# One inference step of a hybrid decoder trunk: the prompt tile with channel-wise projections, two hT buffers, V as loaded operand, probabilities divided on GpSimd

## What is computed

```python
mod = silu(c) @ w_mod + b_mod                      # shift, scale, gate
h = rmsnorm(x, norm_pre) * (1 + scale) + shift
proj = h @ w_in                                    # 1024 -> 2880
qa, ka, va, ga, pb, gb, xc, gc = split(proj)
q, k = rope(qa), rope(ka)                          # A: 8 heads, 2 kv heads, width 64
ya = swa_banded(q, k, va, sinks) * silu(ga)        # window 128, blocks of 128
yb = rwkv7_time_mix(pb, gb, ...)                   # B: 4 heads x 64, delta rule
yc = rglru_mix(xc, gc, ...)                        # C: width 256, conv 4, recurrence
y = concat(ya, yb, yc) @ w_out                     # 1024 -> 1024
x = x + gate * rmsnorm(y, norm_post)
```

## Time and profile before

| | us |
|---|---|
| median of 3 runs | 3261.7 |
| lowest, highest | 3260.98, 3263.45 |
| the profiled execution, its own time | 3271.33 |
| its span (first to last instruction) | 3269.5 |
| DVE busy in it | 1750.7 |
| ACT busy in it | 1429.8 |

### The profile page before, as it was taken

One profiled execution on the slowest core, in us unless ns is written; L12 is line 12 of the kernel. 1 busy time (PEld: TensorE's weight loads), 2 busy tenths in 40 slices (PEclk: granted clock), 3 DMA queues, 4 the chain that ended last, 5 costly groups with the idle time before them and its releaser, 6 DMA issues.

```text
span 3269.5 us, 62255 instructions
## 1 busy us (share of the span) xinstructions
PE 3017.4 (92%) x24404; PEld 1852.7 (57%) x24404; DVE 1750.7 (54%) x4385; ACT 1429.8 (44%) x3055; POOL 0.2 (0%) x4
## 2 busy tenths in 40 slices
PE   4899999999999999998649999999999999999986
PEld 3555556666655555665335555566666655555654
DVE  1455555556555555555414555555566555555554
ACT  0444445445544444544204444454455544445432
POOL 0000000000000000000000000000000000000000
PEclk7999999999999999999769999999999999999996
DMA  9000000000000000000370000000000000000001
GB/s 371 8 20 20 20 20 19 7 20 20 20 13 20 20 20 20 19 7 14 119 289 2 20 20 20 20 19 7 20 20 20 13 20 20 20 20 19 12 9 39
DMA packets 36847, 116.07 MB, mean 36 GB/s; under 512 B 13104, under 2 KB 16304, under 8 KB 36016
## 3 DMA queue, kind: packets, MB, share of 16 engines
q1 hardware_dynamic: 29136, 89.20, 7.8%
q10 hardware_dynamic: 7648, 26.04, 2.1%
HBM read 96.83 MB, written 18.41 MB: 35 GB/s over the span
## 4 chain that ended last, share of the span: by engine, by line
PE 75%; DVE 15%; issue 6%; DMA 2%; ACT 1%; ACTq 0%; DVEq 0%; SPq 0%
PE G L419 37%; PE M L757 14%; PE M L415 5%; PE G L652 4%; DVE small L1367 2%; DMA RB<-in_w_mod 2%; PE M L579 2%; PE M L566 2%; PE G L425 2%; DVE W L1291 1%; DVE RA L1332 1%; DVE Q L1315 1%; PE M L602 1%; PE M L512 1%; PE M L545 1%
## 5 line engine op out<-in xcount | busy, mean ns | idle before, releaser
L419 PE MATMUL G<-w_in,hT 128*128 128x512 f32 (+2 forms) x3072 | 1296.6, 572 | 3.1 <-DVE hT L1212 3.1
L419 PEld LDWEIGHTS G<-w_in,hT 128*128 128x128 f32 x3072 | 571.4, 191 | 552.8 <-issue 474.9
L757 PE MATMUL M<-w_out,yT 128*128 128x512 f32 x1024 | 454.1, 597 | 5.2 <-DVE yT L1446 5.2
L757 PEld LDWEIGHTS M<-w_out,yT 128*128 128x128 f32 x1024 | 191.3, 192 | 223.9 <-issue 223.9
L1224 DVE TENSOR_TENSOR xs<-pB 128x768 f32<-128x768 f32 x32 | 30.7, 959 | 395.8 <-ACT pB L938 395.8
L1315 DVE TENSOR_TENSOR Q<-Q,M 64x256 f32<-64x256 f32 x320 | 133.8, 418 | 119.4 <-PE M L579 115.3
L566 PE MATMUL M<-W 64*64 64x64 f32 x4608 | 163.5, 218 | 7.8 <-DVE W L1291 7.8
L566 PEld LDWEIGHTS M<-W 64*64 64x64 f32 x4608 | 149.4, 135 | 11.3 <-issue 11.3
L630 PE MATMUL M<-kT,stA 64*128 64x256 f32 x512 | 144.3, 402 | 0.0
L652 PE MATMUL G<-Vt,RB 128*128 128x64 f32 x1024 | 127.9, 278 | 0.0
L579 PEld LDWEIGHTS M<-Q,W 64*64 64x64 f32 x2560 | 88.2, 134 | 68.2 <-issue 68.2
(11 more groups left out here) (403 smaller groups left out, 4559.2 us busy)
## 6 DMA issues: line engine op xcount, KB each, us to landing
w_in<-in_w_in SPq DMA_DIRECT2D x2, 11520.0 KB, 33.3
xa<-in_x_prompt SPq DMA_DIRECT2D x16, 512.0 KB, 3.6
RA<-in_w_mod ACTq DMA_DIRECT2D x16, 512.0 KB, 6.3
W<-in_w_mod ACTq DMA_DIRECT2D x16, 512.0 KB, 6.5
w_out<-in_w_out SPq DMA_DIRECT2D x2, 4096.0 KB, 36.7
G<-in_x_prompt SPq DMA_DIRECT2D x16, 512.0 KB, 3.3
x_mid<-RA SPq DMA_DIRECT2D x16, 512.0 KB, 2.8
xa<-x_mid SPq DMA_DIRECT2D x16, 512.0 KB, 3.7
```

The costliest lines, as they stand in the source:

```text
L419: last = mm(out[:, 0:width], hT[:, k, :], Win[:, k, col:col + width], start=k == 0, stop=k == KC - 1)
L757: last = mm(o[:, :], yT[:, k, :], Wout[:, k, 512 * h:512 * h + 512], start=k == 0, stop=k == KC - 1)
```

## The change

The tile is reordered on all engines:

- **Projections.** r, k, v, w/a, xc, gb/gc and ga are made with the weight as loaded operand and 128 columns of hT moving, so that they come out with channels on the partitions: 32 matmuls where there were 8. The 17 transposes and their copies go. q, ka and va stay as they were (ka and va 128 wide, with hT loaded).
- **hT in two buffers**; the loop runs over pairs of tiles. x is scaled in place in xa. x_lo comes after `multiply(5)` and x_hi after `scores(1)`, both into G0; x_hi waits for `hT_lo`, and ACT makes that after `exps(0)`. The projection of gb/gc is taken out of the start of the tile and cut in four (`gates`), behind `right_side(0)`, behind `outputs(0)`, and two behind `outputs(1)`; the first waits for `hT_hi` of the next tile. The gate matmuls of C stand inside the q projection.
- **Front.** `vbT`, `lora`, `kksum` of the next tile stand between the halves of the output projection; the decays (ACT) and operands (DVE) of the next tile follow there.
- **Scores** alternate between the kv heads. **Values**: V (128 x 64) is the loaded operand, 256 columns of probabilities move, kv head 0 goes to partitions 0 to 63 and head 1 to 64 to 127, alternating: 8 matmuls for 16.
- **Division.** The denominators are made and inverted on DVE (`denominators`), GpSimd multiplies the probabilities (128 x 1024 a call) by them, and only then PE transposes them.
- **GpSimd** makes the three roots as powers of -0.5, on 1 or 4 columns.
- Rope moves behind `power_T(2)` on DVE.

The core of the diff:

```diff
+            def channels(out, H, col, width):
+                for k in range(KC):
+                    last = mm(out[0:width, :], Win[:, k, col:col + width], H[:, k, :], start=k == 0, stop=k == KC - 1)
                 return last
...
+                def x_hi(m):
+                    pe.wait_ge(s["hT_lo"], DONE(m))
+                    for k in range(4, 8):
+                        last = T(G0[:, P * (k - 4):P * (k - 4) + P], xa[:, P * k:P * k + P])
+                    last.then_inc(s["xT_hi"], 1)
...
+                    for j in range(4):
+                        last = channels(G0[:, P * j:P * j + P], H, C_R + P * j, P)
+                    last.then_inc(s["rk_mm"], 1)
...
                     def scores(j, ma, mb):
-                        for g, m in ((0, ma), (1, mb)):
+                        for m in (ma, mb):
                             mm(m[:, :].rearrange("p (c k) -> p c k", c=2), identb[:, :], over(mk[:, :], 1, 2),
                                start=True, stop=False, skip_group_check=True)
-                            for c in range(2):
+                        for c in range(2):
+                            for g, m in ((0, ma), (1, mb)):
                                 last = mm(m[:, 256 * c:256 * c + 256], qT[HD * g:HD * g + HD, 2 * j + c, :],
...
                     def values(j):
-                        for k in range(4):
-                            g = k % 2
-                            for f in range(2):
-                                last = mm(G1[:, HD * (4 * j + k):HD * (4 * j + k) + HD], PT[:, f, k, :],
-                                          Vt[:, f, HD * g:HD * g + HD], start=f == 0, stop=f == 1)
+                        for f in range(2):
+                            for g in range(KV):
+                                r = slice(HD * g, HD * g + HD)
+                                last = mm(G1[r, 256 * j:256 * j + 256], Vt[:, f, r], PT[:, f, g::2, :],
+                                          start=f == 0, stop=f == 1)
...
+                    def gates(j):
+                        return channels(G0[:, P * j:P * j + P], H, C_GB + P * j, P)
...
                     scores(1, M0, M1).then_inc(s["s1_mm"], 1)
-                    pe.wait_ge(s["qbd"], DONE(n))
+                    if ahead:
+                        x_hi(n + 1)
+                    pe.wait_ge(s["q_dve"], STEP(n, 5, 5))
                     right_side(0)
+                    if ahead:
+                        pe.wait_ge(s["hT_hi"], DONE(n + 1))
+                    gates(0)
                     solve(0)
-
-                    pe.wait_ge(s["exp0"], DONE(n))
+                    pe.wait_ge(s["pn0"], DONE(n))
                     probs(0, M3, M4).then_inc(s["pT0_mm"], 1)
...
                     exps(0, M3, M4, s["neg0"], s["es0"], s["exp0"])
...
+                    if ahead:
+                        h_lo(n + 1, hT[:, 1 - b])
+                    solved(0)
...
+                    for j in range(2):
+                        pool.wait_ge(s["den%d" % j], DONE(n))
+                        tt(Pm[:, j], Pm[:, j], over(small[:, 24 + 4 * j:28 + 4 * j], 2, 256), ALU.mult)\
+                            .then_inc(s["pn%d" % j], 1)
...
+                    if ahead:
+                        x_mean(n + 1)
                     maxima(0, M3, M4, s["s0_mm"], s["neg0"])
                     product(5)
...
+                    if ahead:
+                        h_hi(n + 1, hT[:, 1 - b])
                     rhs(0)
                     maxima(1, M0, M1, s["s1_mm"], s["neg1"])
+                    denominators(0, s["exp0"], s["den0"])
...
                     rhs(1)
+                    denominators(1, s["exp1"], s["den1"])
```

More of the change, by code:

```diff
@@ L47 @@
 LNX_EPS = 64e-5
+ROOT_D = float(D) ** 0.5
 LRU_C = 8.0
@@ L715, in tile @@
                     outputs(0).then_inc(s["s_mm"], 1)
-                    if ahead:
-                        x_lo(n + 1)
+                    gates(1)
                     pe.wait_ge(s["s_ready"], STEP(n, 1, 2))
@@ new lines, in tile @@
+                    cp(xcb[:, :, 0:3], xcb[:, :, P:P + 3]).then_inc(s["conv_ready"], 1)
+                    dve.wait_ge(s["bonus_mm"], DONE(n))
+                    tt(bonv[:, :], G1[:, 0:256], xsv, ALU.mult).then_inc(s["bonus_out"], 1)
+                    dve.wait_ge(s["gA_mm"], DONE(n))
+                    o = CST["mst"][0]
+                    later = cst[:, o:o + 512]
+                    for r, m in zip(half, (M0, M1)):
+                        last = tt(NW[r], m[r, :].rearrange("p (w u c) -> p w u c", w=2, c=CH), over(nstrict[r], 2, U),
+                                  ALU.mult)
@@ new lines, in tile @@
+                    last.then_inc(s["ntn_ready"], 1)
+                    dve.wait_ge(s["ntn_ready"], DONE(n))
+                    tt(Q[:, :, :], NW[:, 0], over(eye[:, :], 1, U), ALU.add).then_inc(s["q_init"], 1)
+                    dve.wait_ge(s["o_ready"], BEFORE(n))
+                    dve.wait_ge(s["gB_mm"], DONE(n))
+                    for r, m in zip(half, (M3, M4)):
+                        mask = later[r, :].rearrange("p (w c) -> p w c", w=2)[:, :, r]
+                        last = tt(G24[r], m[r, :].rearrange("p (u w c) -> p u w c", w=2, c=CH), over(mask, 1, U), ALU.mult)
@@ new lines, in product @@
+                    def product(level):
+                        dve.wait_ge(s["q_mm5"], STEP(n, level, 5))
+                        for r, m in zip(half, HB):
+                            last = tt(Q[r, :, :], Q[r, :, :], m[r, 256:512].rearrange("p (u c) -> p u c", c=CH), ALU.add)
+                        last.then_inc(s["q_dve"], 1)
+                    power_T(1)
+                    dve.wait_ge(s["gC_mm"], DONE(n))
+                    for r, m in zip(half, HB):
+                        last = tt(G3T[r], m[r, 0:256].rearrange("p (u c) -> p u c", c=CH), over(con("mit")[r, r], 1, U),
+                                  ALU.mult)
@@ L1272, in tile @@
+                    last.then_inc(s["gC_ready"], 1)
+                    product(1)
+                    power_T(2)
                     dve.wait_ge(s["q_out"], DONE(n))
@@ L1461, in tile @@
                     link.end()
[L1463 to L1467 removed]
+                x_mean(l * NT)
+                h_hi(l * NT, hT[:, 0])
+                token_shift(l * NT)
+                operands(l * NT)
+                with dve.Fori(0, NT // 2 - 1) as i:
+                    tile(l * NT + 2 * i, 0, True)
+                    tile(l * NT + 2 * i + 1, 1, True)
+                tile(l * NT + NT - 2, 0, True)
+                tile(l * NT + NT - 1, 1, False)
                 dve.wait_ge(s["o_ready"], BEFORE((l + 1) * NT))
```

622 lines of the change are left out of this document (287 added, 335 removed).

## The result

The changed kernel takes 3387.27 us (median of 4 runs, 3381.66 to 3397.17), the kernel before 3261.34 beside it: a ratio of 1.0388, 95% interval 1.0362 to 1.0414. It is 3.9% slower. The profiled execution took 3397.17 us, its span is 3395.0. The prediction said 3412 (3421 for the profiled execution) and gave slower 0.80.

What follows compares the result with a forecast made beforehand. PE's own work was taken as the bound, 88.2 of 90.46 us a tile. Work 84.8, chain waits 10.3, other idle 0.2 and clock 0.5 made 95.8, +5.3 for 30 tiles: 3412 us, range 3225 to 3530.

Steps and rivals of the forecast that it cites:

- Part 1, PE's work: PE's own work in a tile falls from 88.2 to 84.8 us, by 3.4 us.
- (a): Projections with the weight as loaded operand: 0.1125 us a record, adding 2.4 us of PE work a tile.
- (c): Score matmuls alternating between 64-row halves run side by side: 1.73 us a call, saving 2.06 us a tile.
- the five slots: In a score call, eight records on alternating halves overlap only partly and need 5 slots of 0.213 us.
- (d): Value matmuls on alternating column halves run side by side: 1.07 us a call, saving 1.7 us a tile.
- Part 2, the chain: Between first scores and second probability transposes, PE waits for ACT, DVE and GpSimd: 10.3 us idle a tile.
- Part 3, the clock: Waits of about 3 us halve PE's clock: 0.5 us a tile, bounds 0 and 2.5.
- The start of the chain: The walk over DVE, ACT and GpSimd counts from zero where the first scores end; maxima can't start earlier.
- No pairing of halves: Rival: score and value matmuls on different halves don't run side by side; +1.9 us a tile, 3470 us; chance 0.12.
- The short chain: Rival: GpSimd multiplies at DVE's rate and the clock doesn't fall; +2.4 us a tile, 3325 us; chance 0.15.
- PE stays the bound: Rival: the wait ahead of the second x transposes shrinks; tile 87.0 us, 3150 us, halfway 3205; chance 0.17.
- GpSimd much dearer: Rival: 5 us a product, or slow powers ahead of x; +5 us a tile, 3560 us; chance 0.11.

Runs made afterwards that it cites:

- Experiment 9: Changed kernel with second x transposes in G1, DVE's denominators earlier and second half of hT later, PE's first solve ahead of the first gate projection: 3172.11 us, ratio 0.9725.
- experiment 5: Changed kernel with the old score order, both matmuls of one 64-row half and then both of the other: 3385.38 us, ratio 1.0355.
- experiment 12: Kernel with the other bank, DVE's new order and the solve moved ahead, but the old score order: 3190.65 us, ratio 0.9778.
- experiment 10: Changed kernel with all value matmuls on the lower column half, one head group behind the other, part of the output left out: 3400.43 us, ratio 1.0421.
- experiment 4: Changed kernel with three unused 512-column matmuls put into the wait ahead of the second x transposes: 3413.56 us, ratio 1.0453.
- experiment 11: Changed kernel with unused matmuls put into all three long waits of PE in a tile: 3367.34 us, ratio 1.0324.
- experiment 7: Kernel before with only the score matmuls reordered to alternate between the halves: 3318.43 us, ratio 1.0134.
- experiment 8: Kernel before with its loops over pairs of tiles and nothing else changed: 3263.16 us, ratio 0.9983.

## Why the prediction came out

It was right in sign and near in size: 95.8 us a tile predicted, 94.88 measured. Its steps:

**Part 1, PE's work.** 84.8 us predicted. Experiment 9 shows it: a tile of 87.25 with 2.18 of idle is 85.07. (a) Sixteen records of the first gate projection take 2.05 with the last record's tail, 64 take 7.41 with the tail (7.25 to the next start, 0.113 a record): the predicted 0.1125. (c) 1.67 us a call (1007.14 to 1008.81, the multiply's start less its wait) against 1.73 predicted. That the halves run side by side is right; the five slots are not: in the trace the eight records start in four pairs, 0.01 us apart inside a pair, and so do those of the values (the prediction's 687.33 and 686.87 are 1687.33 and 1686.87 in the earlier trace rows). What (c) is worth was wrong too: counted at -2.06 a tile, it is worth nothing in the changed kernel (experiment 5), and less than half in the repaired one (experiment 12). (d) 1.01 to the next start against 1.07. With its tail a call takes 1.08 where it took 2.00 before; 0.86 of the 0.92 saved are the halves (experiment 10).

**Part 2, the chain.** Counted from the end of the first scores, at 1008.8 in the timeline shown:

| start of | predicted | measured |
|---|---|---|
| second x transposes | 6.25 | 6.5 |
| first gate projection | 8.5 | 8.6 |
| GpSimd's first product | 11.1 | 11.2 |
| first probability transposes | 13.8 | 13.2 |
| GpSimd's product, duration | 2.46 | 1.89 |

Each releaser that was named is there: ACT's hT, DVE's hT, GpSimd. The term of this part that was most mis-sized is the product: 1.89 us, 1.54 times DVE's 1.23 for the same width, not twice. That makes 0.57 less ahead of each group of transposes, 1.1 a tile. The Trainium skill (GPSIMD Engine Reference, section "Performance versus the Vector engine") calls GpSimd about half as fast at such arithmetic, by which the product would take an estimated 2.4; here the measurement decides, and it is better than that. The four waits at the full clock (as experiment 4 shows the third) are 3.08 + 0.85 + 2.12 + 1.68 = 7.7 us where 10.3 was predicted: 1.1 of the difference is the product, 0.8 the waits for the two halves of hT (3.2 and 1.5 predicted), and the 0.7 that is left is spread over small errors of the walk in PE's work and in the starts. All other waits of a tile come to 1.0 (93.83 - 85.07 - 7.73) where 0.2 was kept; the 0.53 ahead of the fifth multiply is half of it. One step was left out: the loop over pairs. The convolution, named as the tightest place with a slack of about 1.5 us, is the one that DVE's 1.8 to 2.1 us at each turn of the loop break through; it was costed at nothing and costs 0.39 a tile on the mean. The small powers on GpSimd (0.57 for one column) stand in no wait of PE's.

**Part 3, the clock.** It falls in every kernel that has the long waits, as the step said, and 2 us of its price fill idle time, as it also said. Predicted 0.5 a tile, measured about 0.7 (experiment 11). In six of the nine tiles it costs just the 0.45 of x_hi on the chain that the step names (p0 at 15.29 and p1 at 23.6 in place of 14.84 and 23.14). The errors go both ways: idle time 1.7 less than predicted, PE's work 0.3, the clock 0.2 and the turn of the loop 0.4 more, together the 0.9 between 95.8 and 94.88. So the mechanism was right, and that the number came out within 1% (3412 against 3387) is in part luck: the errors of the terms cancel.

**The start of the chain** was put at the end of the first scores, and that is only by chance nearly right. DVE comes to the scaling of x at 1009.28 out of its own queue without a gap since 1006.86:

```profile
1006.86 0.85 DVE L1320 TENSOR_TENSOR Q<-Q,M 64x256 f32<-64x256 f32 x2 [0.67 <-PE M L577]
1007.74 0.86 DVE L1357 TENSOR_TENSOR_SCAN lh<-RA,hcar 128x128 f32<-128x128 f32 x2
...
1009.28 0.75 DVE L1213 TENSOR_SCALAR xa<-xa,small 128x1024 f32<-128x1024 f32 x1
1010.06 1.29 DVE L1367 TENSOR_REDUCE small<-M 128x2 f32<-128x512 f32 x2
```

The maxima start at 1010.06 whether the scores end at 1008.8 or, in experiment 5, 1.1 us later (2.92 behind the first mask in both). This is what made the expectations of experiments 5 and 7 miss: I still valued PE's work by its length.

**The rivals.** No pairing of halves: refuted by experiments 5 and 10 in what it says of PE. For the time it would have meant little: nothing for the scores (experiment 5), 13 us for the values (experiment 10), not the 1.9 us a tile that it was priced at. The short chain: about half right on the product (1.89 between 1.23 and 2.46), wrong about the clock. PE stays the bound: this is what experiment 9 makes of the change; its predicted 87.0 a tile for that case stands against 87.25, its 3150 against 3172. GpSimd much dearer: no.

Open: why the clock falls in one tile and not in the next of the same kernel, with the same waits in both. In experiment 9 T is 87.25 or 87.26 in five of nine tiles; a fall of the clock behind the 0.8 and 0.7 us of waits makes it 88.89, a turn of the loop 87.99 and 88.21, both together 89.57. No run tried to find what sets off the fall.

## What to carry to other kernels

On an engine that is 90% busy, a step's work is worth its time only where no other engine's chain runs beside it: mark the starts that are released from outside, and count work inside such a stretch as nothing until the wait in it is filled, and work outside it in full. Before a new operation is put on a slow engine, look at what stands ahead of its inputs in the other queues and at the bank or buffer that its neighbours wait for; here one bank, the order of a few DVE instructions and one solve turned a loss of 3.9% into a gain of 2.7%. Where an extra wait can't be avoided, ask also which work comes behind it, because that work may run at half the clock. And look at every second tile by itself when a loop runs over pairs: a cost that comes once a turn hides in a mean, and here it has the size of half the clock's.

## What the runs showed of the hardware

- Column halves (128 x 64 loaded operands) run side by side whatever the order of issue: 1.08, 1.09 and, on one half alone, 1.94 us for eight records of 256 columns. Row halves (64 x 128) run side by side when they alternate and nothing stands between them: eight records in 1.14 us. With both matmuls of one half, a mask product on the whole array, and both of the other half, four records take 1.13 us; whether the order or the mask product keeps the halves apart is not shown.
- GpSimd multiplies 128 x 1024 float32 by a broadcast operand in 1.89 us, where DVE takes 1.23 for a two-operand instruction of that width; a power of one column takes 0.57 us on GpSimd.
- In the stretches with waits the granted clock went to 0.50, and PE's work of the next 3 to 7 us ran at 1.2 GHz: in all nine tiles of the changed kernel (wait of 3.08 us), in six of nine with waits of 2.12 and 1.68 us (experiment 4), in two of nine with 0.8 and 0.7 us (experiment 9), and in one of ten of the kernel before (0.2 and 0.8 us). Filling one wait of three only moved the fall to a dearer place (+26 us); filling all three kept the clock at 1.00 and made the kernel 20 us faster with 5.6 us more work in each tile.
- A loop body twice as long brought 3.54 in place of 0.62 MB of instructions and up to 2.1 us of idle on DVE at the start of a round. In the kernel before that had no cost in time (experiment 8); in the changed kernel, where a wait of PE hangs on DVE's next instructions, each round was 0.68 to 0.95 us longer.
